# Filling the decay levels of the gated linear attention in pairs of heads, with the diagonal last

## The reference

```python
bc = jnp.cumsum(to_chunks(log_a), axis=-2)
...
diff = bi[:, :, :, None, :] - bi[:, :, None, :, :]
decay = jnp.exp(jnp.where(causal[None, None, :, :, None], diff, -jnp.inf))
att = jnp.einsum('bhid,bhjd,bhijd->bhij', qi, ki, decay)
o_intra = jnp.einsum('bhij,bhje->bhie', att, vi)
```

## Time and profile before

| | |
|---|---|
| median of 3 runs | 532.83 us |
| lowest and highest | 532.58, 533.91 us |
| the profiled execution, its own time | 533.91 us |
| span of its records | 532.2 us |
| TensorE busy | 516.3 us, 97% |
| VectorE busy | 370.7 us, 70% |
| GpSimd, ScalarE busy | 291.2, 236.2 us |
| mean granted TensorE clock | 0.99 |

### The profile page before, as it was taken

One profiled execution on the slowest core, in us unless ns is written; L12 is line 12 of the kernel. 1 busy time (PEld: TensorE's weight loads), 2 busy tenths in 40 slices (PEclk: granted clock), 3 DMA queues, 4 the chain that ended last, 5 costly groups with the idle time before them and its releaser, 6 DMA issues.

```text
span 532.2 us, 7512 instructions
## 1 busy us (share of the span) xinstructions
PE 516.3 (97%) x2806; PEld 417.0 (78%) x2806; DVE 370.7 (70%) x772; ACT 236.2 (44%) x370; POOL 291.2 (55%) x180
## 2 busy tenths in 40 slices
PE   6799999999999999999999999999999999999995
PEld 6776788778888888888888889778777677787883
DVE  3873499859966556656461064999989999869825
ACT  6432844322321244644451445466555554157413
POOL 4371464757734066666414316599999997360701
PEclk9899999999999999999999999999999999989998
DMA  8515166222213002200263403602322222302004
GB/s 262 170 23 188 29 210 199 79 80 81 80 52 108 1 0 81 80 1 1 84 234 108 129 1 108 169 6 81 87 86 80 77 69 88 144 1 79 1 0 158
DMA packets 43642, 46.75 MB, mean 88 GB/s; under 512 B 4432, under 2 KB 32107, under 8 KB 43606
## 3 DMA queue, kind: packets, MB, share of 16 engines
q1 hardware_dynamic: 43606, 46.28, 27.6%
HBM read 44.03 MB, written 2.12 MB: 87 GB/s over the span
## 4 chain that ended last, share of the span: by engine, by line
PE 79%; DVE 11%; issue 4%; ACT 2%; POOL 2%; DMA 1%; SPq 0%; POOLq 0%; ACTq 0%; DVEq 0%
PE bank L1505 29%; PE bank L1525 28%; PE bank L1812 3%; PE bank L1722 3%; PE bank L1649 3%; DVE r_va L1069 2%; PE bank L1699 2%; DVE top L1067 2%; PE bank L1800 2%; PE bank L1711 2%; DMA r_x<-in_x_dram 1%; DVE r_ob L1053 1%; PE bank L1818 1%; POOL w_lo L533 1%; PE bank L1588 1%
## 5 line engine op out<-in xcount | busy, mean ns | idle before, releaser
L533 POOL TENSOR_TENSOR w_lo<-w_raw,w_hi 128x2048 fp32r<-128x2048 f32 (+1 forms) x31 | 140.2, 4526 | 95.0 <-ACT w_hi L682 94.0
L1505 PE MATMUL bank<-hT_hi,w_hi 128*128 128x512 f32 (+1 forms) x280 | 113.5, 405 | 0.8 <-POOL w_lo L533 0.8
L1505 PE MATMUL bank<-hT_lo,w_hi 128*128 128x512 f32 (+1 forms) x280 | 111.0, 396 | 0.0
L1505 PE MATMUL bank<-hT_hi,w_lo 128*128 128x512 f32 (+1 forms) x280 | 110.9, 396 | 0.0
L1525 PE MATMUL bank<-w_hi,hT_hi 128*128 128x512 f32 x252 | 102.0, 405 | 0.1
L1525 PE MATMUL bank<-w_hi,hT_lo 128*128 128x512 f32 x252 | 98.5, 391 | 0.0
L1525 PE MATMUL bank<-w_lo,hT_hi 128*128 128x512 f32 x252 | 98.3, 390 | 0.0
L682 ACT ACTIVATE w_hi<-w_raw 128x2048 fp32r<-128x2048 f32 (+1 forms) x35 | 65.6, 1878 | 37.0 <-PE bank L1525 35.4
L1323 DVE SCALAR_TENSOR_TENSOR bank<-r_va,pvec,bank 128x512 f32<-128x512 f32 x108 | 76.0, 748 | 0.9
L619 POOL TENSOR_TENSOR r_g<-r_g 128x512 f32<-128x512 f32 x48 | 62.0, 1291 | 11.5 <-ACT r_g L863 5.8
L1505 PEld LDWEIGHTS bank<-hT_hi,w_hi 128*128 128x128 f32 (+1 forms) x280 | 52.4, 187 | 14.9 <-issue 2.6
(11 more groups left out here) (226 smaller groups left out, 786.8 us busy)
## 6 DMA issues: line engine op xcount, KB each, us to landing
w_raw<-in_w_in_even_dram SPq DMA_DIRECT2D x14, 1024.0 KB, 5.2
w_raw<-in_w_in_odd_dram SPq DMA_DIRECT2D x16, 512.0 KB, 4.7
w_raw<-in_w_out_even_dram SPq DMA_DIRECT2D x4, 1024.0 KB, 8.3
w_raw<-in_w_in_odd_dram SPq DMA_DIRECT2D x4, 1024.0 KB, 5.1
w_raw<-in_w_out_odd_dram SPq DMA_DIRECT2D x4, 1024.0 KB, 5.0
r_x<-in_x_dram SPq DMA_DIRECT2D x4, 512.0 KB, 6.1
r_x<-bias_rows SPq DMA_DIRECT2D x4, 512.0 KB, 6.0
r_x<-in_x_dram SPq DMA_DIRECT2D x1, 2048.0 KB, 7.9
```

The source lines that it names most:

```text
L533: nc.gpsimd.tensor_tensor(v(w_lo[j % 3]), v(w_raw[j % 2]), v(w_hi[j % 3]).bitcast(F32), ALU.subtract).then_inc(lo_ready, 1)
L1505: ins = nc.tensor.matmul(proj_bank(g)[0:m, :], w[:, k, P * i:P * i + m], h[:, k, :], start=(n == 0), stop=(n == 3 * KC - 1))
```

## The change

Three things change, all of them order; the number and the kind of the computing instructions stay.

The diagonal moves from the front of the level list to its end. So group (7, 1) has no fills any more, and the diagonal is filled last, in slot 11.

TensorE's fills are placed by pairs of heads. In groups (8, 0) to (9, 1) the two pairs of a level stand behind product 8 and product 16, where the whole level stood behind product 12. In slots 10 and 11 one pair stands behind every second half unit, so behind every 12 products: 4, 4, 2, 2 and then 1, 1, 0, 0. `outputs_b` now waits for the last bank of the diagonal.

VectorE empties two banks of a level, does the first half of a top-k round, empties the other two, prepares an operand and does the second half. The diagonal's four banks are emptied after the masks, ahead of the outputs.

```diff
-        FILLS = ["k0", "k1", "kv0", "kv1", "kv2"] + sum((level(lv) for lv in [0] + LEVELS), []) + OB_FILLS
+        FILLS = ["k0", "k1", "kv0", "kv1", "kv2"] + sum((level(lv) for lv in LEVELS + [0]), []) + OB_FILLS
...
-        FILL_IN = {(7, 0): FILLS[0:5], (7, 1): level(0), (8, 0): level(64), (8, 1): level(32), (9, 0): level(16),
-                   (9, 1): level(8)}
-        LEVEL_AFTER = {(10, 3): 4, (10, 7): 2, (11, 3): 1}
+        FILL_IN = {(7, 0): FILLS[0:5], (8, 0): level(64), (8, 1): level(32), (9, 0): level(16), (9, 1): level(8),
+                   10: level(4) + level(2), 11: level(1) + level(0)}
...
-            for f in FILLS[0:5] + level(0):
+            for f in FILLS[0:5]:
                 empty_fill(f)
...
             for i, lv in enumerate(LEVELS):
-                for h in range(BH):
-                    empty_fill((lv, h))
+                empty_fill((lv, 0))
+                empty_fill((lv, 1))
                 topk_half(late + 2 * i)
+                empty_fill((lv, 2))
+                empty_fill((lv, 3))
                 if i + 2 < len(LEVELS):
                     operand(LEVELS[i + 2])
                 topk_half(late + 2 * i + 1)
             topk_masks()
-            for f in OB_FILLS:
+            for f in FILLS[FILL_NO[(0, 0)]:]:
                 empty_fill(f)
...
-                pe.wait_ge(fill_emptied, FILL_NO[(1, BH - 1)] + 1)
+                pe.wait_ge(fill_emptied, FILL_NO[(0, BH - 1)] + 1)
...
-                    [(lambda f=f: whole_level(f[0])) for f in fs if isinstance(f, tuple) and f[1] == 0]
+                    [(lambda f=f: head_pair(f)) for f in fs if isinstance(f, tuple) and f[1] % 2 == 0]
...
-                        if (s_, i) in LEVEL_AFTER:
-                            whole_level(LEVEL_AFTER[s_, i])
+                        if s_ in FILL_IN and i % 2:
+                            head_pair(FILL_IN[s_][i - 1])
```

More of the change, by code:

```diff
@@ L1652, in head_pair @@
                             ins.then_inc(fill_done, 1)
-            def whole_level(lv):
-                head_pair((lv, 0))
-                head_pair((lv, 2))
             def outputs_b(t):
                 n = FILL_NO[f"ob{t}0"]
-                pe.wait_ge(fill_emptied, FILL_NO[(1, BH - 1)] + 1)
+                pe.wait_ge(fill_emptied, FILL_NO[(0, BH - 1)] + 1)
                 pe.wait_ge(fill_emptied, n - 2)
```

## The result

| | before | changed |
|---|---|---|
| median | 532.83 us | 536.95 us (5 runs, 535.61 to 538.33) |
| ratio | | 1.0073, 95% interval 1.0053 to 1.0091 |
| the profiled execution | 533.91 us, span 532.2 | 536.27 us, span 534.5 |
| TensorE, VectorE busy | 516.3, 370.7 us | 517.4, 376.9 us |
| mean granted clock in the profile | 0.991 | 0.997 |

The account below looks back on a forecast made before the run. TensorE's own instructions were taken to set the pace, VectorE having slack. 1.52 us before slot 11's last product plus 2.64 at its end made 4.16, called 4.2: 537.0 us on the 532.83 median, range 535.4 to 538.8.

Parts of the forecast that it names:

- The price of a change of form: TensorE's fills between projection products: a pair of 16 records costs 1.24 us, so a split makes a level 0.35 us dearer.
- The fixed price: Each interruption of TensorE's products by fills: about 0.35 us for going in and coming out, whatever the number of records.
- the 0.34 us behind the first product: Step to the second product after an interruption, 0.228 usual; read as a sign of the fixed price.
- the last product of slot 11: TensorE before the outputs: starts 1.52 us later, from seven splits at 0.35 (2.45 us) less 0.93 for the diagonal.
- The end: Slot 11, before `outputs_b`: the diagonal's second pair and VectorE's emptying add 2.64 us, with 1.4 to 1.6 us showing as a wait.
- VectorE would be ready: Diagonal's last pair, end of slot 11: VectorE has at least 1.6 us in hand, so only its last two copies count.
- nobody would wait at an earlier pair: Pairs before the diagonal's last: operands and banks are ready in time, so TensorE has no wait there.
- the later stages keep the distance: Behind slot 11: every later stage starts 4.2 us late, the delay reaching the end whole.
- free splits: Rival: a half costs half a level, so only the end and the diagonal's moved half count; 1.6 us slower, 534.4; chance 0.08.
- absorption: Rival: a stage behind slot 12 not paced by TensorE's arrival absorbs the whole 4.2 us, leaving 532.8; chance 0.10.
- The clock rival: Rival: the clock falls at the new wait before the outputs, adding 1.6 us, 5.8 in all, 538.6 us; chance 0.14.
- the thin stretch of the earlier trace: Single-column products near 471.72 us, before clock 0.52 at 474.5 to 478: taken as enough to lower the clock without long idling.

Follow-up runs that it names:

- The two kernels over all 128 rows: Kernel before with fills over all 128 rows, whole levels: 542.63 us; the same fills in the first experiment's pair order: 542.82 us.
- the first experiment: Changed kernel with only the splitting into pairs, the diagonal staying first in group (7, 1): 536.67 us, ratio 1.0066 to the kernel before.
- the third: Changed kernel with slot 11's four pairs behind half units 0, 2, 3, 4 instead of 1, 3, 5, 7: 535.35 us, ratio 1.0048.
- the seventh kernel: Kernel before with group (7, 0)'s transposes and state products joined into two interruptions instead of five: 530.92 us, ratio 0.9966.

## Why the prediction was right

The price of a change of form, the step on which most rested, held: a pair between products cost 1.24 us by the earlier trace rows, and it shows as 116.11 to 117.80 less two steps, 1.23:

```profile
116.11 0.39 PE L1506 MATMUL bank<-hT_lo,w_hi 128*128 128x512 f32 x1
116.42 1.11 PE L1650 MATMUL bank<-r_g 64*128 64x64 f32 x16
117.46 0.50 PE L1506 MATMUL bank<-hT_hi,w_lo 128*128 128x512 f32 x1
117.80 0.39 PE L1506 MATMUL bank<-hT_hi,w_hi 128*128 128x512 f32 x1
```

The fixed price is a little low. Over 8 and over 24 interruptions 0.38 us come out for each, not 0.35: the products behind a fill come 0.23 to 0.24 us apart for some five steps, and then every 0.227, which two steps don't catch. And one sign was read wrongly: the 0.34 us behind the first product was taken for the way out of the form, but 0.32 stand there behind fills over all 128 rows as well. The difference of two sums was right; what it was seen in was half right. So the last product of slot 11 was 1.76 us late by the distances (71.16 to 72.92 from the first state product) where 1.52 were forecast. The end was forecast at 2.64 and took 2.66. Together 4.42 instead of 4.16.

That VectorE would be ready held with 2.68 us to spare, more than the 1.6 of the bound. That nobody would wait at an earlier pair held. That the later stages keep the distance held but for the 0.25 us above. The rule of the Trainium skill, TensorEngine Tiling (Array Packing), Key Properties, is that a change of tiling mode drains TensorE. The two kernels over all 128 rows agree in that the change of mode is what costs: 0.03 us for a split without it, 0.38 with it. That the cost is a drain they don't show.

Of the rivals, free splits and absorption have fallen with the first experiment and the distances. The clock rival did not occur in this profile: in the changed kernel the stretch with the new wait, and the one behind the sums of a single column, where the earlier trace rows has 0.52 and which lies 4 us later here, read (us, busy, clock, DMA):

```profile
177.00:182.00 5.00, 3.59 (x36) 1.00 0.00 0
...
478.00:482.00 4.00, 4.00 (x23) 1.00 0.01 4
```

That is why this one execution, at 536.27 us, lies under the 538.1 us that its partner of before suggested. It had no half clock near 475 us, and the stretch from the last layer norm sum to the last product took 58.99 us in it and 60.57 in the profile before, 1.6 us. With the 0.74 us of lead from the other stretch of half clock near 20 us that makes 2.3, and 533.91 + 4.42 + 0.25 - 2.32 is 536.26. The prediction had concluded that the thin stretch of the earlier trace rows was enough to bring the clock down. The same matmuls left it at 1.00 here, so by itself it isn't. The new wait never set the clock down in the profile. Nor do the other executions speak for it: the mean granted clocks of the changed kernel's lay between 0.991 and 0.997, those of the kernel before between 0.990 and 0.998.

That the medians meet the forecast to 0.05 us is luck. By the distances the change costs 4.67 us, half a microsecond above the 4.16 of the sum, and the medians, 4.12 apart, are of few executions with different shares of half clock. At like clocks they say the same as the distances: the changed kernel's three executions at 0.991 took 538.23, 538.33 and 538.69 us, 4.3 to 4.8 above the 533.91 of the profile before, which ran at 0.991 too.

## What to carry to other kernels

Small matmuls that use part of the array's rows or columns should stand together when they are put between full ones: each return trip cost 0.38 us here, whether it carried 8, 16 or 32 records, and no matmul shows a wait for it. Find it in the distances from start to start, with 0.32 us on the way in instead of 0.23, and in the idle time of the weight loads, 0.35 us put down to "issue". And where a step is spread out to give another engine room, look first whether that engine waits already, and keep the last piece some products ahead of its reader.

## What the runs showed of the hardware

Float32 matmuls over all 128 rows with 64 columns go into a row of float32r products (so declared in the kernel; the views print f32 for both) almost free of charge, 0.03 us for a split; over 64 rows it is 0.38. The change between the halved rows and the halved columns, 128*64 to 64*128, took as long as the one back to the full array, 1.46 us with its 24 records in both cases.

Executions differ by how many stretches of half clock they happen to have. Ahead of the last product the ten traces have none (mean clock 0.997), one (0.994) or two (0.991) of them, at two places only: somewhere between 12 and 25 us, and behind the layer norm's sums of a single column at 474 to 481 us. In the runs beside the seventh kernel, the kernel before took 531.19 and 531.22 us where the mean granted clock was 0.996 and 0.998, and 533.99 to 534.09 us where it was 0.990. That spread of 2.9 us is over half of what this change costs. So at a few tenths of a per cent the distances in the traces tell more than the medians: with them the first experiment and the third agree to 0.03 us, while their medians lie 1.3 us apart.
